# First expert layer: token rows turned on chip from raw x tiles and picked by TensorE in blocks of 32

## The reference, cut to what matters

```
x  = x + g1 * y            # y: attention times w_o; each stream has its own g1, shift, scale, g2
h2 = rmsnorm(x, norm2_g) * (1 + scale) + shift            # 512 rows of 1024
lg, le = h2 @ wr_g + b_g, h2 @ wr_e + b_e                 # 4 groups, 32 experts in all
g      = argmax(lg);  e1, e2 = the two best of the group's 8 experts
w      = softmax(lg)[g] * softmax(le[e1], le[e2])
f[tok] = sum over e of w * (silu(h2 @ w_gate[e]) * (h2 @ w_up[e])) @ w_down[e]
x = x + g2 * f
```

```
39 32 34 30 33 35 34 43 35 39 27 38 41 37 29 38 | 32 31 29 27 37 22 22 34 32 33 31 30 26 24 29 21
```

## Time and profile before

| | |
|---|---|
| median of 3 runs | 3088.99 us (3086.84 to 3089.89) |
| the profiled execution | 3092.75 us, its span 3091.4 us |
| mean granted TensorE clock | 0.952 of full speed |
| busy share of the span | TensorE 87%, DVE 23%, ACT 15%, GpSimd 3% |
| DMA | 721 MB, mean 233 GB/s |
| first expert layer | projection 1710 to 1771, norm and router to 1800, first block 1820, last block ends 2353 |
| second expert layer's loop | from 2622 to the end |

### The profile page before, as it was taken

One profiled execution on the slowest core, in us unless ns is written; L12 is line 12 of the kernel. 1 busy time (PEld: TensorE's weight loads), 2 busy tenths in 40 slices (PEclk: granted clock), 3 DMA queues, 4 the chain that ended last, 5 costly groups with the idle time before them and its releaser, 6 DMA issues.

```text
span 3091.4 us, 43046 instructions
## 1 busy us (share of the span) xinstructions
PE 2688.8 (87%) x17970; PEld 1901.5 (62%) x17970; DVE 723.0 (23%) x1844; ACT 462.0 (15%) x1096; POOL 103.8 (3%) x146
## 2 busy tenths in 40 slices
PE   8999999999999999997997868777775998877676
PEld 7888788887888688883445434343433566544454
DVE  2003420022003420023128221000002253332223
ACT  2001310011002310012016120000001142000001
POOL 1001010011001010010000010000001000000000
PEclk9999999999999999998999979989997998999989
DMA  7544765556544765525120169999997214999997
GB/s 266 189 144 146 265 219 181 168 172 204 179 135 164 262 218 195 186 86 202 55 82 1 55 234 398 397 402 398 398 397 262 92 55 171 371 420 419 420 419 310
DMA packets 257036, 721.47 MB, mean 233 GB/s; under 512 B 14207, under 2 KB 141902, under 8 KB 232270
## 3 DMA queue, kind: packets, MB, share of 16 engines
q1 hardware_dynamic: 237760, 691.74, 59.7%
q10 hardware_dynamic: 16782, 18.60, 1.9%
q0 software_dynamic: 2304, 8.39, 0.7%
HBM read 678.84 MB, written 39.85 MB: 232 GB/s over the span
## 4 chain that ended last, share of the span: by engine, by line
PE 71%; DMA 16%; DVE 6%; ACT 3%; issue 3%; ACTq 0%; POOL 0%; SPq 0%; DVEq 0%; POOLq 0%
PE ps L663 18%; DMA arena<-in_moe_w_up 15%; PE ps L674 10%; PE ps L1444 6%; PE ps L2155 5%; PE ps L2468 3%; PE ps L1490 2%; PE ps L2169 2%; PE ps L895 2%; PE ps L687 2%; PE ps L1055 2%; PE ps L1754 2%; PE ps L2429 1%; PE ps L2492 1%; PE ps L2274 1%
## 5 line engine op out<-in xcount | busy, mean ns | idle before, releaser
L663 PE MATMUL ps<-arena 128*128 128x256 f32 x2560 | 568.6, 379 | 3.5 <-DVE arena L745 3.5
L663 PEld LDWEIGHTS ps<-arena 128*128 128x128 f32 x2560 | 482.9, 189 | 73.9 <-issue 4.1
L2155 PE MATMUL ps<-arena 128*64 128x256 f32 x2048 | 259.3, 416 | 78.9 <-issue 77.9
L674 PE MATMUL ps<-arena 128*128 128x256 f32 x1408 | 317.9, 379 | 0.0
L674 PEld LDWEIGHTS ps<-arena 128*128 128x128 f32 x1408 | 264.8, 189 | 46.2 <-issue 8.4
L2155 PEld LDWEIGHTS ps<-arena 128*64 128x64 f32 x2048 | 159.8, 150 | 166.5 <-issue 107.3
L2468 PE MATMUL ps<-arena 128*32 128x128 f32 x4096 | 143.3, 299 | 75.8 <-issue 74.2
L1444 PE MATMUL ps<-arena 128*128 128x512 f32 (+2 forms) x512 | 192.8, 548 | 11.3 <-ACT arena L1391 11.2
L787 DVE TENSOR_TENSOR arena<-arena,ps 128x256 f32<-128x256 f32 x76 | 32.0, 422 | 638.4 <-ACT arena L755 633.8
L2468 PEld LDWEIGHTS ps<-arena 128*32 128x32 f32 x4096 | 128.6, 121 | 85.2 <-issue 83.3
L1444 PEld LDWEIGHTS ps<-arena 128*128 128x128 f32 (+1 forms) x512 | 89.4, 179 | 104.9 <-issue 97.5
(11 more groups left out here) (411 smaller groups left out, 2811.6 us busy)
## 6 DMA issues: line engine op xcount, KB each, us to landing
arena<-in_moe_w_gate SPq DMA_DIRECT2D x64, 2048.0 KB, 31.3
arena<-in_moe_w_up SPq DMA_DIRECT2D x64, 2048.0 KB, 31.1
arena<-in_moe_w_down SPq DMA_DIRECT2D x64, 2048.0 KB, 34.9
arena<-in_mod_w SPq DMA_DIRECT2D x24, 2048.0 KB, 13.4
arena<-in_w_gate SPq DMA_DIRECT2D x44, 1024.0 KB, 5.5
arena<-in_w_up SPq DMA_DIRECT2D x44, 1024.0 KB, 8.1
arena<-in_w_down SPq DMA_DIRECT2D x44, 1024.0 KB, 4.9
expert_in<-arena SPq DMA_DIRECT2D x4, 3328.0 KB, 14.6
```

Of the source, the lines that this page charges most:

```text
L663: last = pe.matmul(k.ps[:, T % 4, off:off + S], w[:, t, T % 2 * P:(T % 2 + 1) * P], h[:, t, :], start=(t == 0), stop=(t == KT - 1), skip_g ...
L674: last = pe.matmul(acc[:, t, :], d[:, T % 2, t * P:(t + 1) * P], k.hid[:, T % 4, :], start=(T == 0 and t % 2 == 0), stop=end, skip_group_c ...
L2155: last = pe.matmul(ps[BL * q:BL * q + BL, b, 0:F], m.xeT[:, t, :], wv[:, t, F * q:F * q + F], start=(t == 0), stop=(t == KT - 1), tile_pos ...
```

## The change

The first expert layer is rebuilt after the manner of the second, and keeps its results in DRAM.

- `BLOCK` becomes (32, 32). With the routing above, 15 of the 32 experts have two blocks and 17 have one: 47 blocks. Of the experts 0 to 13, eleven have two; of all that follow, 15, 20, 23 and 25.
- There is no `expert_in`, no scatter, no row loads and no zeroing of it; `expert_out` has 2048 rows instead of 3072.
- During the projection (`pe_project_picked`) TensorE also takes, for each raw x tile, its share of the logits (8 instruction pairs of 36 columns), of the sum of squares (8 pairs of 1 column) and turns it (4 pairs). ACT squares each tile and scales it by the gain. The norm's factor is applied to the logits and rows afterwards, the shift is added to the rows by GpSimd (`pool_rows`, 8 additions of 128 x 512).
- In the loop each block is picked from the 512 rows (`pe_pick_rows`, 32 pairs), copied out by ACT, turned, copied by DVE; gate and up are 128 pairs of 128 columns, down 32 pairs of 256 columns. ACT copies the result to the single buffer `m.yb` and writes it in 4 transfers of 32 x 256; before the copy it waits until the block before has landed.
- SP no longer waits for the gathers before it loads the next layer's first weights; it waits for the experts 30 and 31 instead.

The core of the diff (kept: the loop's three programs, the picks, the projection on TensorE, the loads):

```diff
-BLOCK = (64, 32)
+BLOCK = (32, 32)
...
+def pe_project_picked(k, m, first, slots, src):
...
+        if j == 1:
+            pe_picked_factors(k, m)
...
+        if j >= 2:
+            pe_token_sums(k, m, j - 1)
+            pe_turn_scaled(k, m, j - 1)
+    pe_token_sums(k, m, KT - 1)
+    pe_turn_scaled(k, m, KT - 1)
...
+def pe_token_sums(k, m, i):
+
+    pe, s = k.nc.tensor, k.s
+    pe.wait_ge(*s["out_added"].at(0, i))
+    for t in range(4):
+        pe.matmul(k.ps[:, 3, 36 * t:36 * t + 36], k.x[:, i, t * P:(t + 1) * P], m.wp[:, t // 2, i, :], start=False, stop=(i == KT - 1), skip_group_check=True)
+    pe.wait_ge(*s["xs_squared"].at(i))
+    for t in range(4):
+        last = pe.matmul(k.ps[:, 3, 144 + t:145 + t], k.sqb[:, i % 4, t * P:(t + 1) * P], k.c["ones"][:, 0:1], start=False, stop=(i == KT - 1), skip_group_check=True)
+    last.then_inc(*s["xs_summed"].up(i))
...
+def pool_rows(k, m):
+
+    pool, s = k.nc.gpsimd, k.s
+    pool.wait_ge(*s["xs_shift"].at(1, 1))
+    for t in range(4):
+        pool.wait_ge(*s["xs_out"].at(t, 1))
+        row = permuted(m.rows[:, t, :], 1)
+        pool.tensor_tensor(row, row, permuted(m.shift_rows[:, t // 2, :], 1), ALU.add).then_inc(*s["rows_made"].up(t, 1))
+    for t in range(4):
+        pool.wait_ge(*s["xs_row"].at(t))
+        row = permuted(m.rows[:, t, :], 0)
+        pool.tensor_tensor(row, row, permuted(m.shift_rows[:, t // 2, :], 0), ALU.add).then_inc(*s["rows_made"].up(t, 0))
...
+def pe_pick_rows(k, m):
+    for t in range(4):
+        for q in range(4):
+            last = k.nc.tensor.matmul(k.ps[32 * q:32 * q + 32, 1, 0:256], m.pick[:, t, :], m.rows[:, t, 256 * q:256 * q + 256], start=(t == 0), stop=(t == 3),
+                                      tile_position=(0, 32 * q), skip_group_check=True)
+    last.then_inc(m.n["x_picked"].sem, 1)
...
         with pe.Fori(first_block(k, m, e, ENG.PE), first_block(k, m, e + 1, ENG.PE)) as g:
-            pe.wait_ge(*m.value("x_ready", g + 1))
-            pe.wait_ge(*m.value("hidden", g))
-            for wv, b in ((wg, 0), (wu, 1)):
+            pe.wait_ge(*m.step("x_ready", g, 1, 1))
+            pe.wait_ge(*m.step("hidden", g, 0, 1))
+            for wv, a in ((wg, 0), (wu, F)):
                 for t in range(KT):
-                    for q in range(G):
-                        last = pe.matmul(ps[BL * q:BL * q + BL, b, 0:F], m.xeT[:, t, :], wv[:, t, F * q:F * q + F], start=(t == 0), stop=(t == KT - 1),
+                    for q in range(4):
+                        last = pe.matmul(ps[BL * q:BL * q + BL, 0, a:a + F], m.xeT[:, t, :], wv[:, t, F * q:F * q + F], start=(t == 0), stop=(t == KT - 1),
                                          tile_position=(0, BL * q), skip_group_check=True)
             last.then_inc(m.n["gated"].sem, 1)
...
+            pe.wait_ge(*m.step("picks", g, 5, 3))
+            pe_pick_rows(k, m)
+            pe.wait_ge(*m.step("x_out", g, 2, 1))
+            pe_turn_picked(k, m)
...
+            act.wait_ge(*m.step("gated", g, 1, 1))
+            act.wait_ge(*m.step("hidden", g, 0, 1))
+            act.activation(m.sil, ps[:, 0, 0:m.F], ACT.Silu).then_inc(m.n["silu"].sem, 1)
+            act.wait_ge(*m.step("x_picked", g, 2, 1))
+            act.activation(m.xe, ps[:, 1, 0:256], ACT.Copy).then_inc(m.n["x_out"].sem, 1)
+            act.wait_ge(*m.step("down", g, 1, 1))
+            act.wait_ge(*m.step("y_out", g, 0, 64))
             act.activation(m.yb, ps[:, 3, 0:W], ACT.Copy).then_inc(m.n["y_ready"].sem, 1)
-            act.wait_ge(*m.value("y_ready", g + 1))
-            for q in range(G):
+            act.wait_ge(*m.step("y_ready", g, 1, 1))
+            for q in range(4):
                 act.dma_start(k.ybuf[bass.ds(g * BL, BL), W * q:W * q + W], m.yb[BL * q:BL * q + BL, :]).then_inc(m.n["y_out"].sem, 16)
...
-    sp.wait_ge(*s["pool_ended"].at(0))
-    for t in range(4):
-        sp.wait_ge(*s[f"gathered{t}"].at(0, 1))
     w = a["b_w_qkv_2"][0]
-    sp_chunk(k, 8, 2, columns(w, 0))
+    sp_chunk(k, 8, 2, columns(w, 0), s["moe_ended"].at(0, "expert", 30))
     sp_chunk(k, 9, 3, columns(w, 512))
     sp_chunk(k, 10, 4, columns(w, D, S))
-    sp_chunk(k, 11, 5, columns(w, D + S, S))
+    sp_chunk(k, 11, 5, columns(w, D + S, S), s["moe_ended"].at(0, "expert", 31))
```

More of the change, by code:

```diff
@@ L282, in second_memory @@
         self.pr = [self.pr2[:, i, :] for i in range(2)] + [sq[:, i * 2 * BANK:(i + 1) * 2 * BANK] for i in range(2)]
-        self.router_cols = (KT + 1) * 36
+        data, where = pack(third_constants())
+        self.third = where, self.nc.inline_tensor(data, "constants_const3").ap()
     def gain(self, i, l):
@@ L1865, in __init__ @@
         self.pick_parts, self.pick = self.small(2, 2, 32), self.small(2, 32)
-        data, where = pack(third_constants())
-        tile = self.small(data.shape[1])
-        self.const3 = tile, k.nc.inline_tensor(data, "constants_const3").ap()
-        self.c = {n: tile[:, a:a + w] for n, (a, w) in where.items()}
+        self.third(k, 264)
         at = k.at.rearrange("p a b -> p (a b)")
@@ new lines, in pe_picked_factors @@
+def pe_picked_factors(k, m):
+    pe, s, ps = k.nc.tensor, k.s, k.ps
+    pe.wait_ge(*s["xs_step"].at("factors"))
+    pe.matmul(ps[:, 3, 0:72], k.c["ones"], m.wsum, start=True, stop=True, skip_group_check=True).then_inc(*s["xs_prepared"].up("bias"))
+    for st in range(2):
+        for half in range(2):
+            pe.matmul(ps[:, 4 + 2 * st + half, :], k.c["ones"], m.shifts[:, st, 4 * half:4 * half + 4, :], start=True, stop=True,
+                      skip_group_check=True).then_inc(*s["xs_prepared"].up(st, half))
@@ new lines, in pe_turn_scaled, with permuted @@
+def pe_turn_scaled(k, m, i):
+    pe, s = k.nc.tensor, k.s
+    pe.wait_ge(*s["xs_scaled"].at(i))
+    if i == 0:
+        pe.wait_ge(*s["xs_shift"].at(1, 1))
+    if i == 4:
+        pe.wait_ge(*s["xs_out"].at(3, 0))
+    for t in range(4):
+        last = pe.transpose(k.ps[:, 4 + t, (i % 4) * P:(i % 4 + 1) * P], m.scaled[:, i % 2, t * P:(t + 1) * P], k.c["ident"])
+    last.then_inc(*s["xs_turned"].up(i))
+def permuted(row, half):
+    return row.rearrange("p (b j a) -> p b j a", b=KT, j=KT)[:, :, 4 * half:4 * half + 4, :]
@@ new lines, in act_router_picked @@
+def act_router_picked(k, m):
+    act, s, l = k.nc.scalar, k.s, m.l
+    act.wait_ge(*s["r_dve"].at(l, "group"))
+    act.activation(m.ge, m.ge, ACT.Exp).then_inc(*s["r_act"].up(l, "group"))
+    act.wait_ge(*s["xs_out"].at(3, 0))
+    for t in range(4):
+        row = permuted(m.rows[:, t, :], 0)
+        act.activation(row, row, ACT.Copy, scale=m.r[:, t:t + 1]).then_inc(*s["xs_row"].up(t))
+    act.wait_ge(*s["r_dve"].at(l, "second"))
+    act.activation(m.m2, m.m2, ACT.Exp).then_inc(*s["r_act"].up(l, "second"))
+    act.activation(k.lnA[:, 1, KT:KT + 1], k.eps, ACT.Silu)
@@ new lines, in dve_router_picked @@
+def dve_router_picked(k, m):
+    V, s, ps = k.nc.vector, k.s, k.ps
+    r = s["r_dve"]
+    for i, name in enumerate(PICKED_BLOCKS):
+        V.memset(m.started[:, i:i + 1], 0.0).then_inc(*m.n[name].up())
+    V.wait_ge(*s["xs_root"].at())
+    V.reciprocal(m.r, m.r).then_inc(*s["xs_step"].up("factor"))
+    V.wait_ge(*s["xs_step"].last())
+    for t in range(4):
+        V.scalar_tensor_tensor(m.lg[:, t, :], ps[:, 3, 36 * t:36 * t + 36], m.r[:, t:t + 1], m.bias2[:, t // 2, :], ALU.mult, ALU.add).then_inc(*r.up())
+    dve_choice(k, m)
```

423 lines of the change are left out of this document (206 added, 217 removed).

## The result

| | kernel before | changed kernel |
|---|---|---|
| device time, median (us) | 3089.89 (3086.84 to 3092.60, 7 runs) | 3099.67 (3093.22 to 3100.43, 7 runs) |
| span of the profiled execution (us) | 3091.4 | 3097.8 |
| first gate product of the first expert layer | 1819.85 | 1817.55 |
| last marker (end of the expert loop) | 2352.84 | 2352.2 |
| last addition of the combination starts | 2380.3 | 2387.3 |

The ratio is 1.0028, with a 95% interval of 1.0016 to 1.0040: slower by some 10 us. The forecast was 3150, 61 us slower; the direction held, the size did not.

A forecast was written before the change was run, and what follows sets the result against it. DMA, moving weights, was taken to bound the kernel before. Front gains included, the loop would end 55.3 us later; 6 lost behind it made +61: 3154 profiled, 3150 as median, range 3075 to 3190 (8 in 10).

The forecast's parts named there:

- Projection: Projection before the expert loop: new work of 2.65 us a tile makes the last product end 14.6 us later, at 1785.4.
- Front: Way from complete sums to first gate matmul: gets shorter, first gate at 1810.4 instead of 1819.85, 9.4 us gained.
- the term of 14.8: Between complete sums and first pick: the later of the GpSimd and DVE chains, taken as 14.8 us.
- Block of 32: TensorE in the expert loop: one block of 32 rows takes 9.65 us, against 13.2 for one of 64.
- Gaps in straight code: TensorE in the expert loop: instruction code arrives late, 1.2 us charged to each expert's first block (0 to 2.3).
- Way back: TensorE's return to the loop's head for second blocks: instruction fetch costs 6 us each, 11 times to expert 13.
- the sentence that the memory might hold the whole body: TensorE's loop: if all 128 KiB of instruction memory counted, returns would cost nothing; free returns had chance 0.26.
- Result buffer: Rival, expert loop: ACT's copy waits for the last result's landing, 12.2 us a block; 3129 with free returns; chance 0.08.
- the rival of the free return: Rival, expert loop: second blocks cost only 9.65 us; 3089, or 3072 if straight gaps go too; chance 0.26.
- Loop from expert 13 on: Expert loop after expert 13: DMA is the bound, 16 transfers of 15.2 us plus 22 blocks' results; 271 us in all.
- Behind the loop: After the last marker: next layer's early weights move beside last results and gathers, 6 us lost (0 to 12).

The follow-up runs named there:

- experiment 5: Changed kernel with GpSimd's eight shift additions replaced by one-column additions on other data (rows lack the shift): 3089.70 us, ratio 1.0009 to the kernel before.
- experiment 1: Changed kernel with a second result buffer and semaphore, even and odd blocks alternating: 3069.02 us, ratio 0.9945 to the kernel before.
- experiment 6: Changed kernel with the next layer's first weights again waiting for this layer's gathers: 3086.42 us, ratio 0.9997 to the kernel before.

## Why the prediction was wrong in size

*Projection*: right in sum, in part by luck. The last product's end was forecast at 1785.4 and measured at 1787.6, with 1.7 of drift. A tile's new work took 2.2 us instead of 2.65, and a tile at a granted clock of 0.75 (1742 to 1751.5) gave 2.3 back; in the execution of experiment 5 no tile was slow, and the way from the first to the last product was 3.3 us shorter.

*Front*: the term of 14.8 was too small; from the complete sums (1792.0) to the first pick (1812.1) it was 20.1. The choice in it took 18.5, and the first gate product came at 1817.55 instead of 1810.4, the 5.5 from the pick to it as forecast; 4.0 us were gained instead of 9.4, within the bounds of 0 to 14. VectorE was taken at 15 from the median of one line beside GpSimd. Experiment 5 showed the additions as the cause. The rule of the Trainium skill (SBUF — State Buffer, Who interferes with whom) that was weighed and not taken, by which an instruction waits out the other engine's whole one, is near to what the rows show: two-input operations of 0.19 us took 0.52 to 1.21 beside additions of 1.26. The row of before held an operation that took 0.41 at best; its median was no measure for one of 0.19.

*Block of 32*: 9.65 forecast, 8.9 to 9.1 from gate to gate where nothing waits (1828.65 to 1837.79, timeline of the changed kernel).

*Gaps in straight code*: 1.2 us to each expert made 16.8 to the end of expert 13; measured were 6.7 (three gaps before gate and up, 5.0 together, and one before the picks, 1.7). With two buffers, where TensorE waits less for others, they were 10.9. So the term was too large by 10. Over the whole loop the profile has 32.7 us of such idle time before gate and up and 7.2 before the picks, but 18.2 of them, before 2216.31, 2294.38, 2309.82, 2325.06 and 2340.39, end where weights have just landed, as the chain shows at the last of them:

```profile
2307.50 31.37 DMA arena<-in_moe_w_up
2338.87 1.52 issue
2340.39 4.63 PE ps L2232 x95
```

What is left is 0.7 us for each of 32 experts.

*Way back*: the step that failed. 6 us on 11 ways made 66 of the 327 us to the end of expert 13; measured were 271 us, and all 11 ways back cost nothing (0.0 us idle before the next gate product). The text had two bounds, 0.2 and 18 us, and took a value from the fetch of two pieces, as if a body longer than one piece could not stay. No row of before showed a loop going round twice, so nothing there could tell; the sentence that the memory might hold the whole body gave the outcome, and got a chance of 0.26. Of the Trainium skill's two statements (Runtime: NRT & Kernel Launch, Instruction fetch mechanics) the window of two pages does not describe this engine: bodies of 900 to 1420 instructions, four to six pages, go back free. Its memory of 128 KiB, which that section gives as 2048 instructions, is near but not met: 1420 stay, 1930 no longer do.

*Result buffer*: the rival that took its place. It was worked out with free returns as 12.2 us a block, 3129; the measured pace was 10.8 a block (271 us for 25). The round trip was sized nearly rightly (13.0 from copy to copy), but charged to every block. With the bound moved off the weights, the stream pauses in every pair, and the result issued at its end lands early. So the buffer cost 29 us to the end of expert 13 (271.0 against 241.9 with two buffers), where the rival had 44 (305 against 261). Its chance of 0.08 was too low because it was weighed with returns of 6 us in place, behind which it would have been hidden.

*Direction*: luck. The change came out slower by a cost that the forecast had put behind another one. The text's condition for a faster kernel, a return below 0.5 us and gaps below 1, was met, and it is faster as soon as the buffer is out of the way: 3069 us in experiment 1, near the rival of the free return with its 3072.

*Loop from expert 13 on*: 271 forecast, 264 measured. *Behind the loop*: 6 forecast, 7.7 measured, and experiment 6 showed that all of it is the early weights. *Sum*: from 61 us, 7.1 are added by the later first gate product (1.7 of it drift). To expert 13 the ways back take off 66, the shorter block 17 (25 x 0.7) and the gaps 10, and 37 are added, the remainder to 271: by the two windows of experiment 1, 21 of them are longer waits for ACT and 13 are products at the lower clock; 3 are not accounted for. The later experts take off 7, and the tail adds 1.7: 6.8, against 6.4 between the spans.

## What to carry to other kernels

When a change frees a loop from one transfer, look at the transfer that is left: its buffer's round trip beside a full stream (13 us here) against the new, shorter block (9 us). Where the trip is longer, a second buffer is the first thing to try (30.5 us here). Before a step is costed with an unseen mechanism, ask for the case in which it costs nothing; a loop body that has been run once may simply still be there. Early loads for the next stage are not free when small transfers on the critical path move beside them (7.8 us here).

## What the runs showed of the hardware

TensorE's loop goes back without cost with a body of up to at least 1420 instructions; at 1930 it fetches 9 to 10 packets of code again and loses 3.5 us on average (5.9 at the first way back), with hardly any weights moving. A transfer of 128 rows of 1 KB had four packets beside its rows when the outer dimension of its destination was four, and landed in 16 us; with an outer dimension of 128 it had 16, and landed in 10.6 beside the same stream. Two-input operations of VectorE of 0.19 us took 0.52 to 1.21 beside GpSimd additions of 1.26, one-input ones (0.19) did not change.
